# A two-layer diffusion backbone on one core: where its modulation products and its first norm are queued

## What is computed

```python
mod = silu(c) @ ada_w[l] + ada_b[l]            # 6 vectors of 1024: shift, scale, gate, twice
h = rms_norm(x, norm_g[l, 0]) * (1 + sc) + sh   # "pre-norm"
y = mixer(h)                                    # attention, DeltaNet, or silu(h@Wg) * (h@Wu) @ Wd
x = x + gt * rms_norm(y, norm_g[l, 1])          # "post-norm"
```

## Time and profile before

| | us |
|---|---|
| three runs | 1295.87, 1300.49, 1300.54 |
| median | 1300.49 |
| the profiled execution, its time | 1299.38 |
| its span in the trace | 1297.6 |
| TensorE busy with matmuls | 1191.1 (92% of the span) |
| VectorE, ScalarE, GpSimd busy | 597.8, 559.6, 118.0 |
| modulation matmuls, 384 records | 50.7 |

### The profile page before, as it was taken

How to read it: one execution, slowest core, us unless ns; L and a number is a source line. 1 busy time by engine, 2 the same in 40 slices (tenths; PEclk the granted TensorE clock), 3 DMA queues, 4 the chain that set the end, 5 groups by cost and what they waited for, 6 DMA issues and landing times.

```text
span 1297.6 us, 18777 instructions
## 1 busy us (share of the span) xinstructions
PE 1191.1 (92%) x7605; PEld 962.1 (74%) x7605; DVE 597.8 (46%) x940; ACT 559.6 (43%) x1020; POOL 118.0 (9%) x110
## 2 busy tenths in 40 slices
PE   5799988999889999999999699997979997999996
PEld 3477734457568888888888367886869976999996
DVE  2532257662453333332223473578756525554444
ACT  2622346663462222223232365664374536444442
POOL 0030220100001111111000000010015100111000
PEclk9899999999889999999999889999969998999998
DMA  9655568892213333333333122233103043666660
GB/s 324 196 174 149 172 222 288 275 273 66 65 52 96 97 97 97 97 94 89 103 93 97 49 66 56 59 82 96 51 3 100 2 114 86 189 181 181 177 179 33
DMA packets 239393, 159.60 MB, mean 123 GB/s; under 512 B 14778, under 2 KB 213836, under 8 KB 239308
## 3 DMA queue, kind: packets, MB, share of 16 engines
q1 hardware_dynamic: 238528, 158.11, 41.3%
q10 hardware_dynamic: 780, 0.29, 0.1%
HBM read 157.33 MB, written 1.05 MB: 122 GB/s over the span
## 4 chain that ended last, share of the span: by engine, by line
PE 84%; DVE 6%; ACT 5%; issue 2%; DMA 2%; POOL 1%; ACTq 0%; DVEq 0%; SPq 0%; POOLq 0%
PE bank L1332 56%; PE bank L1370 4%; PE bank L1359 3%; PE bank L1319 3%; PE bank L1501 2%; PE bank L1409 1%; PE bank L1390 1%; PE bank L1511 1%; PE bank L751 1%; ACT h_work L1627 1%; PE bank L1532 1%; DMA w_raw<-in_ada_w 1%; PE bank L754 1%; PE bank L749 1%; PE bank L1382 1%
## 5 line engine op out<-in xcount | busy, mean ns | idle before, releaser
L1332 PE MATMUL bank<-h_hi,w_hi 128*128 128x512 f32 (+1 forms) x984 | 353.1, 359 | 2.5 <-issue 2.5
L1800 DVE TENSOR_TENSOR w_lo<-w_raw,w_hi 128x1024 fp32r<-128x1024 f32 (+1 forms) x179 | 220.2, 1232 | 289.8 <-ACT w_hi L1594 289.6
L1332 PE MATMUL bank<-h_hi,w_lo 128*128 128x512 f32 (+1 forms) x984 | 348.6, 354 | 0.0
L1332 PE MATMUL bank<-h_lo,w_hi 128*128 128x512 f32 (+1 forms) x984 | 348.4, 354 | 0.0
L1594 ACT ACTIVATE w_hi<-w_raw 128x1024 fp32r<-128x1024 f32 (+1 forms) x179 | 184.3, 1031 | 88.5 <-PE bank L1332 82.3
L1332 PEld LDWEIGHTS bank<-h_hi,w_hi 128*128 128x128 f32 x984 | 186.9, 190 | 28.8 <-issue 3.0
L1332 PEld LDWEIGHTS bank<-h_hi,w_lo 128*128 128x128 f32 x984 | 186.8, 190 | 25.9
L1332 PEld LDWEIGHTS bank<-h_lo,w_hi 128*128 128x128 f32 x984 | 187.1, 190 | 25.5 <-issue 0.5
L1332 PE MATMUL bank<-act_hi,w_hi 128*128 128x512 f32 (+1 forms) x352 | 118.3, 336 | 0.0
L1332 PE MATMUL bank<-act_lo,w_hi 128*128 128x512 f32 (+1 forms) x352 | 118.3, 336 | 0.0
L1332 PE MATMUL bank<-act_hi,w_lo 128*128 128x512 f32 (+1 forms) x352 | 118.3, 336 | 0.0
(11 more groups left out here) (262 smaller groups left out, 1516.8 us busy)
## 6 DMA issues: line engine op xcount, KB each, us to landing
w_raw<-in_ada_w SPq DMA_DIRECT2D x96, 512.0 KB, 5.6
w_raw<-in_ffn_w_gate_up SPq DMA_DIRECT2D x88, 512.0 KB, 3.8
w_raw<-in_ffn_w_down SPq DMA_DIRECT2D x32, 512.0 KB, 4.0
w_raw<-in_gdn_w_in SPq DMA_DIRECT2D x32, 512.0 KB, 4.0
w_raw<-in_attn_w_in SPq DMA_DIRECT2D x14, 512.0 KB, 4.0
w_raw<-in_ffn_w_down SPq DMA_DIRECT2D x16, 384.0 KB, 3.6
w_raw<-in_gdn_w_out SPq DMA_DIRECT2D x8, 512.0 KB, 5.5
w_raw<-in_attn_w_in SPq DMA_DIRECT2D x8, 256.0 KB, 3.5
```

The source lines that it names most:

```text
L1332: m = nc.tensor.matmul(dst, stationary(a, k), moving(b, k), start=(first and k == kk[0] and a == b == 0), stop=(last and k == kk[-1] and a ...
L1800: nc.vector.tensor_tensor(w_lo[where[key] % N_RAW][:, 0:tiles, 0:w], raw_slot(key)[:, 0:tiles, 0:w], w_hi[m % N_SPLIT][:, 0:tiles, 0:w].bi ...
```

## The change

- **Modulation chunks.** 22 of the 62 chunks that stood in attention units leave them: the units whose number is divisible by three, and unit 31, have none now. 2, 3 and 6 chunks stand behind the attention output projection, behind the post-norm's product, and behind the pre-norm's sum of squares, and the same again behind the first FFN. The last batch is split in two; the second half is turned in the DeltaNet sub-layer, behind its third projection. Each chunk keeps its place in the one list, so the weights of the following sub-layer come behind eleven modulation chunks.
- **Splits.** The first two weight chunks of the first FFN and of the DeltaNet sub-layer are no longer split ahead in the sub-layer before but within the pre-norm, between its squares and its root.
- **Start.** Tokens are turned ahead of the parameter rows; VectorE copies x first; it scales x as soon as the root is there, ahead of the modulation's copy and of the first splits.
- **Norm.** `h_hi` of tile 0 is written right behind tile 0's modulation, not behind tile 1's.
- **Last norm.** The second FFN begins with three gate tiles side by side; it was two.

```diff
-ADA_BATCHES = ((0, 4), (4, 12), (12, 24))
+ADA_BATCHES = ((0, 4), (4, 12), (12, 18), (18, 24))
...
+ADA_UNITS = [n for n in range(1, len(ATT_UNITS)) if n % 3][:20]
+GAP_COUNTS = (2, 3, 6)
+ADA_GAPS = {"gap0": 34 + 2 * len(ADA_UNITS), "gap1": 34 + 2 * len(ADA_UNITS) + sum(GAP_COUNTS)}
...
-    if phase == "att" and step:
-        return pair(34, step - 1)
+    if phase == "att" and step in ADA_UNITS:
+        return pair(34, ADA_UNITS.index(step))
+    if phase in ADA_GAPS:
+        a = ADA_GAPS[phase] + sum(GAP_COUNTS[:step])
+        return list(range(a, a + GAP_COUNTS[step]))
...
-    flush = (0, len(ADA_BATCHES) - 1)
-    before = [ada_batch(n) - 1] if first and n and ada_batch(n) - 1 not in flush else []
-    return before, [ada_batch(n)] if last and ada_batch(n) in flush else []
+    before = [ada_batch(n) - 1] if first and ada_batch(n) > 1 else []
+    return before, [0] if last and ada_batch(n) == 0 else []
...
-    out += [("attout", m) for m in range(KT)]
+    out += [("attout", m) for m in range(KT)] + [("ada", a) for a in gap("gap0")]
...
+        if layer == 0:
+            out += [("ada", a) for a in gap("gap1")]
...
+        LAST_DOWN = [("down", 0, KT - 1, 2), None]
...
-                split_to(ahead(("attout", m)))
+                split_to(ahead(("attout", m), ("attout", KT - 1)))
...
+                if n == 2:
+                    turn_rows(len(ADA_BATCHES) - 1)
...
+                    take_mods(len(ADA_BATCHES) - 1)
                     dve.wait_ge(gate_exp, 1)
...
-                dst = take(("mod", batch), "att" if batch == 1 else "work")
+                dst = take(("mod", batch), "att" if batch in (1, 2) else "work")
...
-                project_two(i, lo, [("gate", layer, n) for n in range(2)])
+                together = 2 + layer
+                project_together(i, lo, [("gate", layer, n) for n in range(together)], (P,) * together)
                 for n in range(1, 2 * FT):
-                    if n > 1:
+                    if n >= together:
                         project(("gate", layer, n), ("gate", layer, n), lo)
...
-            pe.wait_ge(rows_in, 16 * ROW_DMAS)
-            for n, (rows, count) in enumerate(((rowsA, R_N), (rowsB, 2 * 6 * KT), (rowsC, 4 * 3 * GH))):
-                dst = take(("cols", n))
-                finish(nc.tensor.transpose(dst[:, 0:count], rows[0:count, :], ident[0:count, 0:count]),
-                       ("cols", n))
             pe.wait_ge(tok_in, 16 * 2)
             for k in range(KT):
                 dst = take(("x", k))
                 for t in range(4):
                     m = nc.tensor.transpose(dst[:, t * P:(t + 1) * P], tok[:, t, k * P:(k + 1) * P], ident)
                 finish(m, ("x", k))
+            pe.wait_ge(rows_in, 16 * ROW_DMAS)
+            for n, (rows, count) in enumerate(((rowsA, R_N), (rowsB, 2 * 6 * KT), (rowsC, 4 * 3 * GH))):
+                dst = take(("cols", n))
+                finish(nc.tensor.transpose(dst[:, 0:count], rows[0:count, :], ident[0:count, 0:count]),
+                       ("cols", n))
...
+            ada(ada_after("gap0", 0))
             post_norm(0)
+            ada(ada_after("gap0", 1))
             pre_norm(1)
+            ada(ada_after("gap0", 2))
             ffn(0)
+            ada(ada_after("gap1", 0))
             post_norm(1)
             if LAST_SUB == 3:
+                ada(ada_after("gap1", 1))
                 pre_norm(2)
-                gdn_tensor(pe, take, finish, project, project_two, project_whole, to_tokens)
+                ada(ada_after("gap1", 2))
+                gdn_tensor(pe, take, finish, project, project_together, project_whole, to_tokens, turn_rows)
...
-                if i:
-                    split_to(split_no[FIRST_CHUNK[i]] + 1)
                 for k in range(KT):
                     x_ready(act, i, k)
                     if k >= 4:
                         wait_product(act, ("pre_sq", i, k - 4))
                     nc.scalar.activation(pre_sq[:, k % 4, lo:T], xT[:, k, lo:T],
                                          ACT.Square).then_inc(pre_sq_ready, 1)
+                if i:
+                    split_to(split_no[FIRST_CHUNK[i]] + 1)
...
-                    if k:
-                        act.wait_ge(h32_ready, i * KT + k)
-                        nc.scalar.activation(h_hi[:, k - 1, lo:T], h_work[:, k - 1, lo:T],
-                                             ACT.Copy).then_inc(h_hi_ready, 1)
+                    for m in {0: [0], 1: []}.get(k, [k - 1]):
+                        act.wait_ge(h32_ready, i * KT + m + 1)
+                        nc.scalar.activation(h_hi[:, m, lo:T], h_work[:, m, lo:T], ACT.Copy).then_inc(h_hi_ready, 1)
                     if k == KT - 3:
                         split_to(ahead(FIRST_CHUNK[i]))
...
-                    split_to(ahead(("down", layer, m, 2)))
+                    split_to(ahead(("down", layer, m, 2), LAST_DOWN[layer]))
...
+            def scale_x(i, k):
+                lo = first_token(i)
+                nc.vector.tensor_tensor(h_work[:, k, lo:T], xT[:, k, lo:T], pre_rstd[:, lo:T],
+                                        ALU.mult).then_inc(pre_scaled, 1)
+
             def pre_norm(i):
                 lo = first_token(i)
                 split_to(split_no[FIRST_CHUNK[i]] + 1)
                 wait_evacuated(dve, ("pre", i))
                 for k in range(KT + AHEAD):
-                    if k < KT:
-                        nc.vector.tensor_tensor(h_work[:, k, lo:T], xT[:, k, lo:T], pre_rstd[:, lo:T],
-                                                ALU.mult).then_inc(pre_scaled, 1)
+                    if k < KT and i:
+                        scale_x(i, k)
...
+            for k in range(KT):
+                wait_product(dve, ("x", k))
+                release(nc.vector.tensor_copy(xT[:, k, :], bank(("x", k))), ("x", k))
...
+            wait_evacuated(dve, ("pre", 0))
             for k in range(KT):
-                wait_product(dve, ("x", k))
-                release(nc.vector.tensor_copy(xT[:, k, :], bank(("x", k))), ("x", k))
+                scale_x(0, k)
             ada(ada_after("start", 0))
...
                 pre_norm(2)
-                gdn_vector(dve, link, split_to)
+                ada([ADA_N - 1])
+                gdn_vector(dve, link, split_to, take_mods)
```

15 lines of the change are left out of this document (9 added, 6 removed).

## The result

The changed kernel takes 1292.31 us (median of six runs, 1290.41 to 1292.74), the kernel before on the same chip 1297.22 (six runs). The ratio is 0.9945 with a 95% interval of 0.9924 to 0.9966, thus about 7.1 us less, a small gain that the interval keeps apart from none. The profiled execution took 1290.41; its span is 1288.7 against 1297.6, 8.9 less, and TensorE's mean granted clock is 0.974 (0.965 before). The forecast was 1291.0, or 8.4 less than the profiled execution of before.

The account below looks back on a forecast made before the run. TensorE, holding 84% of the chain, was taken as the bound, through its waits and work on the path. Terms -3.7 - 6.3 - 0.3 - 0.5 + 0.7 + 1.7 = -8.4 from 1299.38 gave 1291.0 us, own range 1287.5 to 1295.

Parts of the forecast that it names:

- Start, -3.7: Start of the kernel: new load order and early scaling of x let ScalarE modulate at 39.9, not 43.65; -3.7 us.
- Attention, -6.3: Attention units: eleven lose a chunk pair, mostly gaining in grouped-query tiles and at the end; -6.3 us, bounds -11.7 and -4.
- Rival 3: Differential attention tiles: clock falls to the low level for whole tiles, 8.4 more a tile, 1316 us; chance 0.04.
- Output projection, forecast 0: Attention output projection up to the post-norm's product: no change in time forecast, 0.
- First gap, -0.3: Before the first FFN: chunks delay nothing, splits cost +0.65, the last h_lo pair bounds the end; -0.3 us.
- Second gap, -0.5: Before the DeltaNet sub-layer: half of 0.96 from the post-norm's product at a higher clock, splits 0; -0.5 us.
- DeltaNet, +0.7: DeltaNet sub-layer: one more turn, 1.07, which covers a 0.36 wait for the gates; +0.7 us, bounds 0 and +1.5.
- Last norm, +1.7: Second FFN's start: fourth gate tile's w_hi waits for the first tile's buffer behind three tiles; +1.7 us, bounds 0 and +3.3.
- Sum, -8.4: Whole kernel: the six terms add to -8.4 against the profiled execution's 1299.38, giving 1291.0 us.
- Rival 1: Whole kernel: all moved work was on the path, attention -11.7 instead of -6.3, 1285.6 us; chance 0.12.
- Rival 2: Whole kernel: gains given back in first gap, DeltaNet and last norm, attention -5, total -1.2, 1298.2 us; chance 0.18.
- the other signs named in the prediction: First projection matmul at 41 to 43.5, no DMA hole at 22, longer differential turn waits, pause about 1.7 before fourth gate tile.

Follow-up runs that it names:

- e2: Kernel before with only the start of the change (tokens turned ahead of parameter rows, VectorE scaling x early), no chunks moved; ratio 0.9964 to the kernel before.
- e1: Changed kernel with two gate tiles side by side at the start of the second FFN instead of three; ratio 0.9924 to the kernel before.
- e6: Changed kernel with h_hi of tile 0 again written behind tile 1's modulation, in all four pre-norms; ratio 0.9975 to the kernel before.
- e7: Changed kernel with its 22 late modulation chunks behind gate tiles 2 to 23 of the first FFN, none in the gaps; ratio 1.0169 to the kernel before.
- e9: Changed kernel run again without alteration, for a second profile; ratio 0.9960 to the kernel before.
- e10: Changed kernel with four w_hi buffers and seven raw ones, three gate tiles kept side by side; one run, 1309.13 us.
- e3_dense_units: Changed kernel with its twenty pairs of modulation chunks in attention units 1 to 20 instead of all but each third; ratio 0.9936 to the kernel before.

## Why the prediction was right

- **Start, -3.7: right**, by size and by what ends last, the second split. The first product is at 18.56 (forecast 18.2), the second split 1.5 earlier, ScalarE's modulation at 39.88 (39.9). The root came 1.1 later than forecast and the scaling held the copy to `ada_rows` up by 1.2; 0.2 of room was left, so this is partly luck. In other executions the start gained 2.0 to 3.6. That the first projection matmul moves by more and that this is lost again also came true, as e2 shows.
- **Attention, -6.3: right as a sum of waits, 1.6 short in this execution.** The same program without that low stretch (e1) takes 116.49 instead of 122.77: -6.28. Unit 16 to the end gave -4.94, where my terms for unit 18 (-0.8), for 21, 24 and 27 (-2.9), for the turn (+1.07) and for the end (-2.2) make -4.8. Units 0 to 16 gave -1.34, forecast -1.45, but here errors cancel, as these two profiles (before and e1) show by tile: unit 6's tile gave 0.68 (forecast 0.4), unit 15's 0.36 (0.2), and the tile that batch 1's `take_mods` and turn leave or enter 0.25 instead of 0.85. Without that `take_mods` TensorE gets past the wait for VectorE 0.5 earlier in the tile, not 0.95. What failed is the clock: I gave the fall a chance of 0.04 because I thought of whole tiles. It came in short stretches, one or two to an execution, worth 1.6 each, in five of seven profiles with this placement. Rival 3 had the right mechanism with a price fifteen times too high. The missing term is about +1.6 on average (seven stretches in seven profiles).
- **Output projection, forecast 0: missed by -1.6.** Before, the clock was low for its first matmuls; in the profiled execution after, it wasn't. I take this for the clock's chance and not for the change: of the twelve profiles with the changed order five take 45.94 and the others 47.3 to 47.6. The two errors of the clock cancel, so the total looks better than the steps.
- **First gap, -0.3: right** (-0.28), with its parts a little off: splits +0.32 for my +0.65, the first matmul 0.45 earlier in all, and 0.17 of it given back in the FFN. The new order moves the first matmul by 0.84 and gives all of it back (e6).
- **Second gap, -0.5: undersized, -1.79.** The post-norm's product ran at full clock: -0.95, of which I took half. That product was also at full clock without chunks (e2, e7), so most of it was chance in the kernel before, not the change's merit. The other 0.84 is the new order of `h_hi`, which I counted in the first gap only. It moves the first matmul and is given back by the `gates` matmul (e6).
- **DeltaNet, +0.7: near** (+0.96, and +1.09 in e9), but made up otherwise. To the `gates` matmul it takes 1.40 longer: 0.98 is what the order gives back, 0.42 is the turn, less the wait of 0.36, which is gone as forecast. From there to the post-norm's product it took 0.45 less, within what executions of one program differ by.
- **Last norm, +1.7: right in sign and place, undersized, and its cause only half right.** The pause is there, 2.01, and e1 takes it away. But the buffer alone is not the cause: with a fourth one the pause stays (e10). The order of ScalarE's list is a second condition, which I didn't read. The split starts 0.3 later for the same reason, since the silu of tile 0 goes first. The 0.37 from the new order came (0.35). The rest of the excess is the low clock behind the pause, against a shorter loss by it in the kernel before: from the first matmul on it takes 192.50 with two tiles at full clock (e1), 193.20 before and 195.48 after.
- **Sum, -8.4: right, with luck.** The profiled execution hit it (-8.9) because errors of the clock met: +1.6 in attention, -1.6 in the output projection, and in the second gap -0.95 where half was counted. By medians the change gave 7.1.
- **Rivals.** Rival 1 is out: attention gave 4.7 to 6.3, and VectorE's waits took up the rest. Rival 2 had the right list of what is given back, but all three at their upper bounds; measured were +2.05, +0.96 and -0.28. Its attention of -5 is nearer to the -4.66 of this execution than my -6.3. The first output-projection matmul came 8.3 earlier, not 10, by the clock's 1.6; the other signs named in the prediction are there (the DMA share at 22 to 24 is 1.06, and TensorE has no new wait at turn in a grouped-query tile until the last one, where it is 1.35 for 0.75), and none of its two refutations (no pause, attention shorter by over 9).

## What to carry to other kernels

Ask of each piece of filler which wait it stands in. Here a pair of modulation chunks in a differential tile cost nothing in the first unit, 0.4 in the fourth and 0.7 to 0.85 in the third (the first tile's third unit apart, where it cost nothing); in a grouped-query unit it cost 0.98, until three of a tile's four were gone and VectorE was the bound. Taking filler out of the units that wait gave next to nothing, and in five of seven profiles the clock fell there. Keeping it there and taking it out of the others was worth another 3.7 to 3.9, of which 1.6 is the low stretch in the changed kernel's two profiles. Ask also whether filler shares the engine with its like: two chunks side by side cost what one costs alone. An earlier first matmul is no gain as long as a later operand paces the tile, so look for where an earlier start is given back. When more tiles go side by side, look at every condition of the next tile's operand, the free buffer and the place in the list of the engine that makes it: freeing the buffer alone changed nothing.

## What the runs showed of the hardware

**The clock's low stretches are much of the noise of this kernel.** Nothing in the DeltaNet sub-layer differs between e3_dense_units and the changed kernel, yet it took 341.73 and 331.21. Windows of after, and then of e3:

```profile
780.00:820.00 40.00, 37.65 (x299) 31.09 (x299) 10.44 (x12) 25.86 (x42) 0.00 (x0) 0.96 0.16 40
820.00:840.00 20.00, 20.00 (x112) 17.32 (x111) 17.53 (x24) 9.16 (x13) 0.00 (x0) 1.00 0.31 79
```

```profile
780.00:820.00 40.00, 37.98 (x265) 31.06 (x264) 10.44 (x12) 19.49 (x35) 0.00 (x0) 0.76 0.16 40
820.00:840.00 20.00, 20.00 (x97) 16.83 (x96) 11.29 (x15) 12.32 (x15) 0.00 (x0) 0.89 0.21 53
```

The same list of instructions, with TensorE busy throughout in both, ran at 0.96 and 1.00 or at 0.76 and 0.89. A gain of a few microseconds can therefore not be read off one span; cut at the same instructions, many stretches repeat within 0.1 (the first FFN takes 364.18 to 364.24 in eight profiles with the changed norm). What decides which of the two a run gets stayed open.

**A lone modulation chunk costs TensorE 1.20 in the gate tiles, a pair 0.98 in the attention units.** The records of a pair, on four strips of the bank, start four at a time, those of a lone chunk two at a time, and either way the next product starts 0.97 to 0.98 after the first record. A change from products of rounded halves to plain 32-bit matmuls and back adds some 0.2.
